# First output projection by token: three of its four column groups multiplied with the tokens as rows and turned to channels through DRAM

## The reference

```python
# first block, pool mixer (D = 2048, T = 256)
h = rms_norm(x) * (1 + scale) + shift              # scale, shift, gate from c @ w_mod
u, g = split(h @ w_in)
y = (grouped(window_mean(u) - u) * pool_scale) * silu(g)
x = x + gate * (y @ w_out)                         # the first output projection
h = rms_norm(x) * final_norm_g
# second block, gated delta net, then banded attention
hn = rms_norm_2(h, norm_w[0])
proj = hn @ a_w_in                                  # reads every channel of x
...
```

## Time and profile before

| | us |
|---|---|
| runs | 1333.16, 1334.98, 1335.25 (median 1334.98) |
| the profiled execution, its own time | 1334.82 |
| its span, first to last instruction | 1332.7 |
| TensorE busy | 1326.0 (99%) |
| VectorE busy | 960.7 (72%) |
| ScalarE busy | 732.5 (55%) |
| GpSimd busy | 196.8 (15%) |

### The profile page before, as it was taken

How to read it: one execution, slowest core, us unless ns; L and a number is a source line. 1 busy time by engine, 2 the same in 40 slices (tenths; PEclk the granted TensorE clock), 3 DMA queues, 4 the chain that set the end, 5 groups by cost and what they waited for, 6 DMA issues and landing times.

```text
span 1332.7 us, 18992 instructions
## 1 busy us (share of the span) xinstructions
PE 1326.0 (99%) x6963; PEld 1109.1 (83%) x6963; DVE 960.7 (72%) x1279; ACT 732.5 (55%) x1091; POOL 196.8 (15%) x313
## 2 busy tenths in 40 slices
PE   9999999999999999999999999999999999999999
PEld 5445999988888888888888988888888888888887
DVE  4558999988779898999676668746666566666552
ACT  2213435456766657556688775465655646565431
POOL 0000012100001000032122200002234234232000
PEclk9999999999999999999999999999999999999999
DMA  9999989885676776599866676656879889789662
GB/s 383 394 416 371 353 345 408 299 279 181 202 248 207 239 226 222 182 294 293 222 181 198 201 236 224 194 186 205 260 236 270 261 271 283 217 278 262 179 197 83
DMA packets 90354, 339.36 MB, mean 255 GB/s; under 512 B 12368, under 2 KB 12768, under 8 KB 85792
## 3 DMA queue, kind: packets, MB, share of 16 engines
q1 hardware_dynamic: 67392, 261.30, 57.7%
q0 software_dynamic: 22880, 76.94, 19.0%
HBM read 310.91 MB, written 29.38 MB: 255 GB/s over the span
## 4 chain that ended last, share of the span: by engine, by line
PE 81%; DMA 12%; DVE 5%; issue 1%; ACT 1%; SPq 0%; POOL 0%; DVEq 0%; POOLq 0%
PE acc L905 19%; PE acc L848 14%; PE acc L849 14%; PE acc L850 14%; PE acc L909 10%; DMA mod_ring<-mod_w 7%; DMA raw<-weights 5%; PE misc L1174 2%; DVE w_lo L1903 1%; PE misc L905 1%; PE misc L1164 1%; DVE mod_ring L1873 1%; PE misc L1065 1%; DVE mod_late L1873 1%; DVE gate_ring L1873 1%
## 5 line engine op out<-in xcount | busy, mean ns | idle before, releaser
L1903 DVE TENSOR_TENSOR w_lo<-raw,w_hi 128x1024 fp32r<-128x1024 f32 x392 | 471.5, 1221 | 178.7 <-ACT w_hi L1339 173.1
L1339 ACT ACTIVATE w_hi<-raw 128x1024 fp32r<-128x1024 f32 x392 | 405.4, 1054 | 321.6 <-DMA raw<-weights 234.7
L848 PE MATMUL acc<-w_hi,b_op 128*128 128x512 f32 x704 | 277.1, 394 | 0.0
L849 PE MATMUL acc<-w_lo,b_op 128*128 128x512 f32 x704 | 274.3, 390 | 0.0
L850 PE MATMUL acc<-w_hi,b_op 128*128 128x512 f32 x704 | 274.3, 390 | 0.0
L905 PE MATMUL acc<-b_op,w_hi 128*128 128x512 f32 x640 | 162.1, 395 | 0.0
L850 PEld LDWEIGHTS acc<-w_hi,b_op 128*128 128x128 f32 x704 | 132.2, 188 | 27.5
L848 PEld LDWEIGHTS acc<-w_hi,b_op 128*128 128x128 f32 x704 | 132.4, 188 | 26.3
L849 PEld LDWEIGHTS acc<-w_lo,b_op 128*128 128x128 f32 x704 | 132.4, 188 | 26.1
L905 PEld LDWEIGHTS acc<-b_op,w_hi 128*128 128x128 f32 x640 | 115.2, 189 | 21.0 <-issue 0.2
L905 PE MATMUL acc<-a_op,w_hi 128*128 128x512 f32 x448 | 113.1, 394 | 0.3 <-DVE a_op L1913 0.3
(11 more groups left out here) (314 smaller groups left out, 2012.8 us busy)
## 6 DMA issues: line engine op xcount, KB each, us to landing
raw<-weights SPq DMA_DIRECT2D x392, 512.0 KB, 5.1
mod_ring<-mod_w SPq DMA_DIRECT2D x26, 1024.0 KB, 14.4
u_ring<-weights SPq DMA_DIRECT2D x32, 512.0 KB, 14.6
gate_ring<-weights POOLq DMA_DIRECT2D x30, 512.0 KB, 8.3
mod_late<-mod_w SPq DMA_DIRECT2D x6, 1024.0 KB, 6.4
head_d<-head POOLq DMA_DIRECT2D x32, 128.0 KB, 4.3
t<-head_d POOLq DMA_DIRECT2D x32, 128.0 KB, 5.9
z_d<-z POOLq DMA_DIRECT2D x28, 128.0 KB, 4.8
```

The source lines that it names most:

```text
L848: nc.tensor.matmul(to, xh[:, t], wh, start=kt == 0, stop=False)
L849: nc.tensor.matmul(to, xh[:, t], wl, start=False, stop=False)
L1339: nc.scalar.activation(w_hi[:, m.c % HL_SLOTS], raw[:, q.c % RAW_SLOTS], ACT.Copy).then_inc(own.up(s_hi), 1)
L1903: nc.vector.tensor_tensor(w_lo[:, slot], raw[:, q.c % RAW_SLOTS], w_hi[:, slot].bitcast(F32), ALU.subtract).then_inc(own.up(s_lo), 1)
```

## The change

Groups `G_WOUT` to `G_WOUT+2` are multiplied `by_token`, each into a pair of banks of its own (acc 0, acc 1, misc 0); `G_WOUT+3` stays `joined`. The sums of the three groups are copied by ScalarE (`out_by_token`) to `y_part`, transposed by VectorE (`out_turned`), taken through DRAM by GpSimd, and added to x from SBUF (`gated`: 4 `scalar_tensor_tensor`). There is one `y_part` and one `y_32`: `out_by_token(j)` waits for `s_x1 >= j`, which is the end of `gated(j - 1)`. `early_sums` moves behind the sixth slab of `G_A`, where `last_sums` now stands too. In the first by-token group TensorE takes kt in plain order. The weights of the three groups are laid out as plain slabs on the host. In the diff the first `out_turned` is GpSimd's (its first call stands behind the four `x_again` loads), the second VectorE's.

```diff
+        y_part = vo[:, 8:12].rearrange("p k t -> p (k t)")
+        y_32 = at("y_32", [P, 4 * T], F32, vo_at + 12288)
...
+            def out_turned(j):
+                n = turn_of("y", j)
+                pool.wait_ge(s_head_32, n)
+                to_dram(y_32[:], z_d, s_head_d)
+                pool.wait_ge(s_head_d, 64 * n)
+                from_dram(z_d, y_part, s_z_t)
+            out_turned(0)
             pool.dma_start(head_rows[:], rows_d.to_broadcast([P, 2 * P])).then_inc(s_rows, 16)
             pool.wait_ge(s_opnd, O_Z)
             pool.dma_start(ab_raw[:], w_ab_d.rearrange("p k c -> p (k c)")).then_inc(s_ab, 16)
+            out_turned(1)
+            out_turned(2)
...
-                        pe.wait_ge(s_free, u - U_WOUT + 1 if g < G_WOUT + 3 else u - 1)
+                        pe.wait_ge(s_free, U_WOUT + 2 * (h + 1) if g == G_WOUT + 3 else u - 1)
...
-            for j in range(4):
-                joined(G_WOUT + j, a_op, ready=None if j else lambda kt: O_H + kt // 4 + 1,
-                       fillers={6: early_sums} if j == 3 else None, order=PLAIN if j else SPLIT)
+            for j in range(3):
+                pe.wait_ge(s_free, j + 1)
+                group(None, slab_of(Num(G_WOUT + j)), pair_of_banks(j), 0, a_hi, a_lo, products=by_token,
+                      ready=None if j else lambda kt: O_H + kt // 4 + 1)
+            joined(G_WOUT + 3, a_op)
...
-            joined(G_A, b_op, ready=operand_b, fillers={4: last_sums, 6: decay_and_beta}, order=SPLIT)
+            def all_sums():
+                early_sums()
+                last_sums()
+            joined(G_A, b_op, ready=operand_b, fillers={5: all_sums, 6: decay_and_beta}, order=SPLIT)
...
+            def out_by_token(j):
+                act.wait_ge(s_used, slab_of(Num(G_WOUT + j + 1)).c)
+                if j:
+                    act.wait_ge(s_x1, j)
+                to = y_part.rearrange("p (m a c) -> p a m c", m=GM, a=2)
+                src = acc[:, j] if j < 2 else misc[:, 0:2 * GC]
+                for half in range(2):
+                    of = src[:, half * GC:(half + 1) * GC].rearrange("p (m c) -> p m c", m=GM)
+                    nc.scalar.activation(to[:, half], of, ACT.Copy).then_inc(own.up(s_zs if half else s_act), 1)
+            out_by_token(0)
+            hi_parts(Num(N_WOUT + AHEAD), SLABS)
...
+                elif j == 2:
+                    hi_parts(n + 7, 1)
                 else:
-                    hi_parts(n, SLABS)
+                    out_by_token(j + 1)
+                    hi_parts(n + SLABS, SLABS if j == 0 else SLABS - 1)
...
+            def out_turned(j):
+                n = turn_of("y", j)
+                dve.wait_ge(s_zs, n)
+                for _ in range(2):
+                    dve.sem_inc(own.also(s_free), 1)
+                if j:
+                    dve.wait_ge(s_head_d, 64 * (n - 1))
+                nc.vector.transpose(y_32[:], y_part).then_inc(own.up(s_head_32), 1)
+            def gated(j):
+                dve.wait_ge(s_z_t, 64 * turn_of("y", j))
+                dve.wait_ge(s_x_again[j], 16)
+                for m in range(GM):
+                    kt = 4 * j + m
+                    nc.vector.scalar_tensor_tensor(
+                        out=xres[:, kt], in0=vo[:, 8 + m], scalar=modv[:, 2 * KT + kt:2 * KT + kt + 1],
+                        in1=xres[:, kt], op0=ALU.mult, op1=ALU.add
+                            ).then_inc(own.up(s_x1 if m == GM - 1 else s_dve), 1)
+            lo_parts(Num(N_WOUT + 9), 6)
+            dve.wait_ge(s_gate, GATES)
+            out_turned(0)
+            lo_parts(Num(N_WOUT + AHEAD), SLABS - 1)
             for j in range(4):
-                gated_half(j, 1)
+                if j == 3:
+                    gated_half(3, 1)
+                else:
+                    gated(j)
+                    dve.wait_ge(*own.last())
...
-                if j < 3:
-                    lo_parts(n, 4)
-                    gated_half(j + 1, 0)
-                    lo_parts(n + 4, 4)
+                if j < 2:
+                    lo_parts(n + 7, 1)
+                    out_turned(j + 1)
+                    lo_parts(n + SLABS, SLABS - 1 if j == 0 else 4)
+                    if j == 1:
+                        gated_half(3, 0)
+                        lo_parts(n + 12, 2)
+                elif j == 2:
+                    lo_parts(n + 6, 2)
```

More of the change, by code:

```diff
@@ L153 @@
            ("q", 3), ("k", 3), ("v", 2), ("z", 2), ("v", 3), ("z", 3))
-TURNS = tuple([("va", v) for v in range(4)] + [("za", 0), ("za", 1), ("za", 2)] +
+TURNS = tuple([("y", j) for j in range(3)] + [("va", v) for v in range(4)] + [("za", 0), ("za", 1), ("za", 2)] +
               [of for of in B_ORDER if of[0] in "qk" or of in (("z", 0), ("z", 1), ("z", 2))])
@@ L652, in _, with to_dram, from_dram @@
                 x_again(j)
+            def to_dram(tile, through, written):
+                for a in range(4):
+                    rows = tile[32 * a:32 * a + 32].rearrange("p (n c) -> p n c", c=P)
+                    pool.dma_start(through[:, :, a], rows).then_inc(written, 16)
+            def from_dram(through, tile, done):
+                for b in range(4):
+                    of = through.rearrange("x n a c -> x (n a) c")[:, :, 32 * b:32 * b + 32]
+                    pool.dma_start(tile[32 * b:32 * b + 32].rearrange("p (k t) -> p k t", t=32), of
+                                   ).then_inc(done, 16)
+            def out_turned(j):
[5 more added lines that the diff above has]
+            out_turned(0)
             pool.dma_start(head_rows[:], rows_d.to_broadcast([P, 2 * P])).then_inc(s_rows, 16)
@@ L704, in _ @@
                 query_parts(j)
-            def to_dram(tile, through, written):
-                for a in range(4):
-                    rows = tile[32 * a:32 * a + 32].rearrange("p (n c) -> p n c", c=P)
-                    pool.dma_start(through[:, :, a], rows).then_inc(written, 16)
-            def from_dram(through, tile, done):
-                for b in range(4):
-                    of = through.rearrange("x n a c -> x (n a) c")[:, :, 32 * b:32 * b + 32]
-                    pool.dma_start(tile[32 * b:32 * b + 32].rearrange("p (k t) -> p k t", t=32), of
-                                   ).then_inc(done, 16)
             def first_gate_turned(j):
@@ L896, in joined @@
                     if part == 0:
-                        pe.wait_ge(s_free, u - U_WOUT + 1 if g < G_WOUT + 3 else u - 1)
-                    tiles = [(part * SLAB_J + kk, sums_of(u)[:, m * GC:(m + 1) * GC],
+                        pe.wait_ge(s_free, U_WOUT + 2 * (h + 1) if g == G_WOUT + 3 else u - 1)
+                    tiles = [(part * SLAB_J + kk, acc[:, u % 2, m * GC:(m + 1) * GC],
                               slice(kk * HALF + m * P, kk * HALF + (m + 1) * P))
@@ L1612, in first_tap_v @@
             def first_tap_v(v):
[L1614 removed]
+                act.wait_ge(s_z_t, 64 * turn_of("va", v))
                 act.wait_ge(*own.last())
@@ L2080, in gated_half @@
                         nc.vector.scalar_tensor_tensor(
-                            out=xres[:, kt], in0=sums_of(u)[:, (2 * m + part) * T:(2 * m + part + 1) * T],
+                            out=xres[:, kt], in0=acc[:, u % 2, (2 * m + part) * T:(2 * m + part + 1) * T],
                             scalar=modv[:, 2 * KT + kt:2 * KT + kt + 1], in1=xres[:, kt], op0=ALU.mult, op1=ALU.add
@@ L2085, in gated_half @@
                 dve.sem_inc(own.also(s_free), 1)
-            lo_parts(Num(N_WOUT + 9), 3)
-            gated_half(0, 0)
-            lo_parts(Num(N_WOUT + 12), 3)
-            for j in range(4):
-                gated_half(j, 1)
+            def out_turned(j):
[19 more added lines that the diff above has]
+            lo_parts(Num(N_WOUT + AHEAD), SLABS - 1)
+            for j in range(4):
+                if j == 3:
[3 more added lines that the diff above has]
+                    dve.wait_ge(*own.last())
                 for m in range(GM):
@@ L2457, in _ @@
                         if j < 3:
-                            dve.wait_ge(s_z_t, 64 * (j + 5))
+                            dve.wait_ge(s_z_t, 64 * turn_of("za", j))
                         else:
-                            dve.wait_ge(s_zs, 8)
+                            dve.wait_ge(s_zs, turn_of("za", 2) + 1)
                         add(o, o, gate_z[j][:], ALU.mult, done=s_tmp)
@@ L2684, in build_stream @@
         b.append(joined_slabs(m, column) if (kind, j) == ("z", 3) else slabs(m, [column]))
-    rest = np.concatenate([g, grp, joined_stage(i["pool_w_out"][0], quarters), joined_stage(a, order_a[:8]),
+    rest = np.concatenate([g, grp, slabs(i["pool_w_out"][0], quarters[:3]),
+                           joined_slabs(i["pool_w_out"][0], quarters[3]), joined_stage(a, order_a[:8]),
                            *[slabs(a, [c]) for c in order_a[8:15]], joined_slabs(a, order_a[15]),
```

8 lines of the change are left out of this document (1 added, 7 removed).

## The result

1357.9 us, the median of five runs (1355.5 to 1358.4), against 1333.6 (1333.2 to 1335.3) for the kernel before on the same chip: a ratio of 1.0172 (95% interval 1.0161 to 1.0183), so 24.3 us slower. The forecast had the sign and the mechanism, but 12.7 us of it and a range that ended at 1356: the change costs almost twice what was worked out.

A forecast was written before the change was run, and what follows sets the result against it. TensorE's own work was taken to bound the kernel. Waits of 5.3, 8.2 and 1.6 us less a gain of 2.3 gave 12.8, alike S - 36.8 = 12.7; added to 1334.8 this forecast 1347.5 us, range 1341 to 1356.

The forecast's parts named there:

- I take 16.5 for each: Length chosen for each of the three turns through DRAM, near the complete one of 17.6 us but below it.
- S: Sum of the three serial turns through DRAM, put at 49.5 us; the delay was to be S - 36.8 = 12.7.
- T: One turn through DRAM, from start of the transpose to data landed; bounds 13.6 to 21.5 us.
- The timetable: Chain from the first transpose at 278.4 through three turns to G_A+1 at 328.4 + S, 377.9 against 365.21 before.
- I take 0: Loss from TensorE's clock falling behind the wait of 8.2 us: bounded by 0 and 8, counted as 0.
- rival (b): The serial chain, and TensorE's clock falls: 2.8 to 5.6 us more for one or two slabs, 1350 to 1353; chance 0.20.
- The gain: On TensorE, 24 projection slabs at 2.72 for 2.80 us save 1.9, the a_op stall 0.4: together 2.3 us.
- Just in time: gated_half(3, 0) on VectorE ends at 334.6, before TensorE starts G_A at 335.2.
- Rival (e): Weights run short: TensorE waits for slab 70's w_lo if the first two turns exceed 37.5 us; 1353 to 1360; chance 0.05.
- (a): The same serial chain with quick turns of 13.6 to 15.3 us each, 4 to 9 us slower; chance 0.15.
- (c): The turns through DRAM are hidden, a small gain; all of it, 1332.5, needs turns of 11.5 us; chance 0.05.
- (d): No measurable change: the three turns sum to 34 to 39 us, so gain and wait cancel; chance 0.05.

The follow-up runs named there:

- 10th kernel: 9th kernel, with SyncE also holding the weights' DMAs from slab 35 on until the third turn has landed: 1349.4 us.
- 3rd kernel: Changed kernel with ScalarE's copy and VectorE's transpose of the next group put ahead of the squares and lo_scaled: 1348.1 us.
- 9th kernel: Changed kernel with weight slabs 35 and 36 behind the third turn's data, 37 and 38 behind gated_half(3, 1), as control: 1352.1 us.
- experiment 7: Changed kernel with the 24 DMAs of the turns issued from ScalarE's queue in place of GpSimd's: 1359.8 us.
- clock kept (2): Changed kernel plus spare matmuls into an unread bank that fill most of TensorE's long waits: 1355.1 us.
- half bytes (8): Changed kernel with half of each turn's bytes left out in both directions, as many DMAs as before: 1346.6 us.
- nobody waits (1): Changed kernel with the values back from DRAM unused and not waited for, all copies, transposes and DMAs kept: 1338.5 us.
- experiment 11: Changed kernel with copy and transpose first, first turn early, gated_half(3, 1) sooner, and three fewer weight slabs between transpose and gated: 1339.9 us.

## Why the prediction fell short

**The term that was mis-sized: "I take 16.5 for each", S = 49.5.** Measured 20.3, 19.2 and 19.4, S = 58.9. The 9.4 us more, by the prediction's own sum, make 22.1 in place of 12.7. The range took in S up to 53 and ended below it; the bounds of T (13.6 to 21.5) had held the value. What failed is how a value was chosen between them: the rows were weighed by the DMA share of their slice, and by which other tensor was on the way. The share ranks them badly: the leg of 7.5 us lies in a slice of 9 like that of 11.4, and the changed kernel's legs of 9.6, 8.5 and 8.2 fall where the slices of before read 8, 5 and 6. What goes with a leg's length is the traffic that moves while it lasts, here mostly weights. In the trace of before, the write leg of 6.5 us went beside 1.12 MB of weights, that of 7.5 beside 1.55 and that of 11.4 beside 2.26 (the last two beside 0.53 and 1.05 MB of other tensors as well). The chosen stretch moves 1.7 to 2.3 MB in a write leg:

| leg | weights moved in it, MB | us |
|---|---|---|
| write, 10th kernel, third turn | 0.35 | 5.2 |
| write, 3rd kernel, second and third | 0.44, 0.41 | 5.0, 5.2 |
| write, changed kernel, second, third, first | 1.67, 1.99, 2.27 | 8.5, 8.2, 9.6 |
| read, 10th kernel, third turn | none | 5.3 |
| read, 9th kernel, third turn | 0.61 | 5.7 |
| read, changed kernel, the three | 1.32, 1.70, 1.62 | 9.2, 9.2, 9.6 |
| read, 3rd kernel, third turn | 2.36 | 11.9 |

The first write leg of the changed kernel had 0.5 MB of `x_again` beside it too. The table alone does not show which is cause and which effect, since a longer leg also lets more weights pass. Experiment 10 does, for the third turn: against its control it only holds weights, and the write leg falls from 8.1 us (1.95 MB) to 5.2 (0.35 MB). The read leg was short in the control already (5.7, 0.61 MB), where full slots of `raw` held the weights. With experiment 7 (another queue, little change) and 8 (half the bytes, 4 us less a turn) it leaves no other cause for most of the difference; for the first two turns that is concluded from the third. Moving a turn does not help where the weights only wait for the next leg, as experiment 3 shows: write legs short, read legs long, T the same.

**The timetable held.** `G_A+1` was to start at 328.4 + S. In kernels that keep the changed kernel's lists, later than before by (forecast S - 36.8):

| kernel | S | S - 36.8 | measured |
|---|---|---|---|
| changed | 58.9 | 22.1 | 23.3 |
| clock kept (2) | 57.6 | 20.8 | 19.2 |
| other queue (7) | 60.6 | 23.8 | 24.5 |
| half bytes (8) | 46.5 | 9.7 | 9.6 |
| nobody waits (1) | 40.5 | 3.7 | 3.4 |

(In runs 1 and 7 S is VectorE's list, as no `gated` waited for the DMA.) The first transpose came 1.2 to 2.1 us before the forecast's 278.4, and where the clock fell its 2 us are in the measured column; the two nearly cancel. So the serial chain, the single buffer behind it and the count of three were right; `gated(j)`, squares, copy and transpose followed each other as told.

**The clock.** "I take 0" was wrong, by 2.0 us. The trace of before had no such idle stretch to show it, and the mechanism was written down as rival (b), at 2.8 for one slab where 2.0 were measured. That a slab slowed ahead of VectorE's next event would be hidden was right too; it held for two of the three. The Trainium skill (TensorE: Matmul & The Clock Gate, Why this matters for your kernels) warns that an idle gap between bursts drops the engine to half rate: the trace agrees, each of the three waits (3.8, 5.9 and 5.5 us) has a slab at 1.2 GHz behind it, and the loss is 2 us and not three times that only because the path ran over VectorE.

**The gain** was as told: slabs of (312.10 - 246.79) / 24 = 2.72 us, no stall for the third part of `a_op`, about 2.3 us.

**"Just in time" was not.** `gated_half(3, 0)` was forecast at 334.6, TensorE's want at 335.2. It began at 338.32 and ended at 340.0: two turns longer by 6.5 together, less the 1.2 of the early start. This wait of 3.8 was new, but is the same lateness met sooner, and adds nothing to the end.

**Rival (e)** came in part: the first two turns took 39.5 together, over its 37.5, TensorE waited 1.45 us at 332.29 for the `w_lo` of slab 70, and 1357.9 lies in its 1353 to 1360. But that wait was the same lateness met earlier, and hidden; what made the time was the length of the turns. **Rivals (a), (c), (d)** did not come. And (c) was priced wrongly: no turn, however quick, would have given 1332.5. Experiment 1 gives 1338.5, since the slabs between transpose and `gated` take 13 us by themselves and the folds stand ahead of `gated_half(3, 1)`.

The parts: 12.7 forecast, + 9.4 for the turns, + 2.0 for the clock, - 1.2 for the earlier start, is 22.9 of 23.3 measured; of the other 0.4, 0.2 are the sums (375.88 to 377.43, 1.55 in place of 1.35), and 0.2 stay open.

## What to carry to other kernels

When a step is put on the critical chain through DRAM, price each leg beside the traffic that will run with it, in MB moved during the leg, and not by the best or the nearest row of elsewhere; here the same leg of 0.5 MB took 5.2 us beside 0.35 MB of weights and 8.2 beside 2.0. Count how often the term stands in the sum before choosing a value between its bounds: with a factor of three the range must reach to the slow bound. And what a serial buffer costs is not only the turn: the list of the in-order engine behind each release (here slabs, folds and squares) still cost 4 us with turns of no length, and putting it in another order gave back 18.8 of the 24.3 us (experiment 11), where holding back the weights during one turn gave 2.7 beyond its control (10) and another queue nothing (7).

## What was not expected of the hardware

Two legs of the same size, by the code one writing pieces of 512 bytes and one reading pieces of 128, took the same time with the engines nearly free (5.2 and 5.3 us). One DMA of 128 KB, of the same pattern and from the same queue, took 2.6 or 4.9 us (medians of four) by what else was on the engines. GpSimd's legs show as 192 packets each; from ScalarE's queue (experiment 7) the same 0.52 MB show as 1088 packets in the third write leg and 4160 in the second read leg, and those legs were no slower. The granted clock stood at half for one slab (5.3 us) behind a wait of 3.8 us, and came back to full within the next (0.85 over its first 2.1 us).
